# A hybrid encoder layer on one core: the first two projection blocks from scaled rows, the shift's part added in PSUM, and a quarter of the other conditioning sums on GpSimd

## What is computed

```python
cond = silu(c)                                        # 1024 numbers
sh1, sc1, gt1, sh2, sc2, gt2 = split(cond @ ada_w + ada_b, 6)      # ada_w: 1024 x 6144
h = rmsnorm(x, norm1_g) * (1 + sc1) + sh1
q, k, v, feat, gl = split(h @ w_in, ...)              # w_in: 1024 x 4736
# attention from q, k, v; RWKV-7 scan both ways from feat; gates from gl; mix; x = x + gt1 * mixed
h = rmsnorm(x, norm2_g) * (1 + sc2) + sh2
# 16 experts pick 64 tokens each; x = x + gt2 * moe; final rmsnorm
```

## Time and profile before

| | value |
|---|---|
| median of three runs | 1517.89 us |
| the profiled execution | 1520.18 us, span 1518.1 us |
| granted TensorE clock, mean | 0.979 of 2.4 GHz |
| PE busy | 1390.5 us, 92% |
| DVE busy | 445.7 us, 29% |
| ACT busy | 212.5 us, 14% |
| POOL busy | 39.9 us, 3% |
| bytes by DMA | 483.49 MB, mean 318 GB/s |

### The profile page before, as it was taken

The page is one execution under the profiler, slowest core; times in us unless marked ns, Lnnn a source line. Parts: engine busy times, 40 slices in busy tenths (PEclk is TensorE's granted clock), DMA queues, the critical chain, the costliest instruction groups (busy, mean ns, idle before and its releaser), DMA issues.

```text
span 1518.1 us, 21694 instructions
## 1 busy us (share of the span) xinstructions
PE 1390.5 (92%) x9319; PEld 650.0 (43%) x9319; DVE 445.7 (29%) x821; ACT 212.5 (14%) x436; POOL 39.9 (3%) x49
## 2 busy tenths in 40 slices
PE   5999999999999996999999799799799899889897
PEld 2444544445777554343353253253253243243232
DVE  2799554852347314112102102102102101100202
ACT  2035002331332011110010010010010010010011
POOL 2001230000000000000000000000000000000000
PEclk9999999999999997999999999999999999999999
DMA  9954142263215548999999999999999999999996
GB/s 347 371 196 112 56 112 83 84 171 99 83 59 196 192 212 309 364 425 427 428 427 427 428 429 428 428 428 428 428 428 429 428 428 429 429 429 428 428 425 279
DMA packets 95223, 483.49 MB, mean 318 GB/s; under 512 B 36443, under 2 KB 53933, under 8 KB 64949
## 3 DMA queue, kind: packets, MB, share of 16 engines
q1 hardware_dynamic: 95101, 482.49, 78.7%
q10 hardware_dynamic: 56, 0.01, 0.0%
HBM read 470.93 MB, written 10.50 MB: 317 GB/s over the span
## 4 chain that ended last, share of the span: by engine, by line
PE 67%; DMA 26%; DVE 2%; issue 2%; SPq 1%; ACT 1%; POOL 1%; DVEq 0%; POOLq 0%
PE psum L1257 16%; DMA arena<-in_exp_w_up_dram 13%; DMA arena<-in_exp_w_gate_dram 11%; PE psum L651 10%; PE psum L1274 9%; PE psum L739 7%; PE psum L1216 4%; PE psum L1138 3%; PE psum L1054 2%; PE psum L1381 2%; PE psum L1298 1%; SPq L294 1%; DMA arena<-in_ada_w_dram 1%; PE psum L786 1%; PE psum L863 1%
## 5 line engine op out<-in xcount | busy, mean ns | idle before, releaser
L1257 PE MATMUL psum<-arena 128*64 128x512 f32 x2048 | 468.4, 614 | 68.9 <-DMA arena<-in_exp_w_up_dram 51.3
L1257 PEld LDWEIGHTS psum<-arena 128*64 128x64 f32 x2048 | 159.5, 141 | 369.3 <-issue 355.3
L1274 PE MATMUL psum<-arena 128*64 128x512 f32 x928 | 202.7, 593 | 8.0 <-issue 6.5
L651 PE MATMUL psum<-arena 128*128 128x512 f32 x336 | 147.2, 598 | 1.4 <-DVE arena L1762 1.4
L1274 PEld LDWEIGHTS psum<-arena 128*64 128x64 f32 x928 | 76.1, 137 | 126.7 <-issue 126.0
L739 PE MATMUL psum<-arena 128*128 128x512 f32 x256 | 122.0, 610 | 0.0
L651 PEld LDWEIGHTS psum<-arena 128*128 128x128 f32 x336 | 63.8, 192 | 82.2 <-issue 79.5
L2173 DVE TENSOR_TENSOR arena<-arena,psum 128x512 f32<-128x512 f32 x32 | 19.9, 682 | 255.9 <-PE psum L1257 255.9
L2191 DVE TENSOR_TENSOR arena<-psum,arena 128x1024 f32<-128x1024 f32 x7 | 8.6, 1225 | 252.7 <-PE psum L1274 252.7
L2165 DVE TENSOR_TENSOR arena<-arena,psum 128x512 f32<-128x512 f32 x32 | 19.9, 682 | 176.6 <-ACT arena L1650 176.6
L1636 ACT ACTIVATE arena<-psum,arena 128x128 f32<-128x128 f32 x64 | 24.4, 457 | 316.9 <-PE psum L1216 316.9
(11 more groups left out here) (312 smaller groups left out, 1114.3 us busy)
## 6 DMA issues: line engine op xcount, KB each, us to landing
arena<-in_exp_w_gate_dram SPq DMA_DIRECT2D x64, 2048.0 KB, 23.8
arena<-in_exp_w_up_dram SPq DMA_DIRECT2D x58, 2048.0 KB, 26.6
arena<-in_exp_w_down_dram SPq DMA_DIRECT2D x52, 2048.0 KB, 27.0
arena<-in_ada_w_dram SPq DMA_DIRECT2D x24, 1024.0 KB, 9.8
arena<-in_exp_w_down_dram SPq DMA_DIRECT2D x20, 1024.0 KB, 17.8
arena<-in_w_in_dram SPq DMA_DIRECT2D x16, 1024.0 KB, 5.8
arena<-in_exp_w_up_dram SPq DMA_DIRECT2D x12, 1024.0 KB, 6.9
arena<-in_x_dram SPq DMA_DIRECT2D x2, 2048.0 KB, 8.6
```

Source lines behind the costliest of these rows:

```text
L651: ins = mm(bank(b % 4), by(w_ring[g % 2], KC)[:, k, j * P:(j + 1) * P], by(hT, KC)[:, k, :], start=(k == 0), stop=(k == KC - 1))
L1257: ins = mm(bank(4 * kind + n)[e * 64:(e + 1) * 64, :], by(xeT, KC)[:, k, e * 64:(e + 1) * 64], row_half(j + e, r, first)[:, n * 512:(n + 1 ...
L1274: ins = mm(bank(4 + n)[e * 64:(e + 1) * 64, :], by(hidT, FBLK)[:, 4 * kk + b, e * 64:(e + 1) * 64], by(ring[(j + e) % RING], 4)[:, b, n * ...
```

## The change

1. `h_scaled` (x transposed times the scale) is written by DVE without the shift, and blocks 0 and 1 are projected from it. ACT adds the shift and writes `hT`, eight instructions, for blocks 2 and on.
2. SP loads the scale half of `ada_w` first (four loads of 1 MB, 256 rows by 1024 columns each), then `w_in` group 0 into a place of its own, then the four loads of the shift half. PE's `mod_first` takes the scale half alone, 256 columns for each column tile.
3. DVE sums the shift half over its eight row blocks (`shift_sum`), PE adds up over partitions with eight products of one column, DVE adds the bias. DVE then sums `w_in` group 0 weighted by the shift (`bias_sum`, 256 columns, eight instructions), PE adds up with two products of one column, and ACT adds the two results to PSUM banks 0 and 1. `shift(0)` and `shift(1)` wait for it.
4. Pieces 11, 15, 19 and 23 are summed by POOL: four products with a scalar, and two additions of 128 x 2048. The loads of 15, 19 and 23 wait for POOL. DVE keeps twelve pieces. `ada_pool` needs a second set of products with ones, in the same column tiles and banks.
5. On PE, blocks 7 and 8 go ahead of the sums with ones. ACT's `kk_sq` waits for them, since it writes where `ada_pool[0]` lies.
6. All eleven parameter loads (one is new, `ada_b` for shift and scale) are issued by ACT; SP starts with `x`. ACT loads the table for Sqrt ahead of the squares. The four broadcast loads of `ada_b` go.

```diff
-            for r, src in param_rows[:5]:
-                load(par_rows[r:r + src.shape[0], :], src, "params_in")
             load(by(x_in, TT), x[0].rearrange("(t p) d -> p t d", p=P), "x_in")
+            def first_piece(i, o):
+                src = ada_w[0, 2 * i * P:2 * (i + 1) * P, o:o + D].rearrange("(k p) n -> p k n", p=P)
+                load(by(ada_ring[i], 2), src, f"ada_in{i}")
             def ada_piece(n):
-                if n >= 4:
-                    sp.wait_ge(sem("ada_used"), n - 3)
+                if n < 12:
+                    sp.wait_ge(sem("ada_used"), n - 7)
+                elif n >= 12 and n in ADA_POOL:
+                    sp.wait_ge(sem("pool_prep"), ADA_POOL.index(n))
+                elif n >= 12:
+                    sp.wait_ge(sem("ada_used"), 4 + ADA_DVE.index(n - 4) + 1)
...
-            for n in range(KC):
-                ada_piece(n)
-            for q in range(4):
-                load(adab_first[quarter(q), :], ada_b[0:1, 512 * q:512 * (q + 1)].partition_broadcast(32), "first_in")
+            for i in range(4):
+                first_piece(i, D)
             weights(0)
+            for i in range(4):
+                sp.wait_ge(sem("mod_mm"), i + 1)
+                first_piece(i, 0)
             weights(1)
...
+            for q, n in enumerate(ADA_POOL):
+                pool.wait_ge(sem("ada_in3"), 16 * (n // 4 + 1))
+                acc, k = ada_pool[q // 2], n % KC
+                if q == 0:
+                    pool.wait_ge(sem("proj_mm"), 2)
+                    pool.wait_ge(sem("hT_ready"), 2 * KC)
+                    pool.wait_ge(sem("modT_ready"), 4)
+                if q % 2 == 0:
+                    s(nc.gpsimd.tensor_scalar(acc, rest_ring[3], cond[:, k:k + 1], None, ALU.mult))
+                else:
+                    s(nc.gpsimd.tensor_scalar(rest_ring[3], rest_ring[3], cond[:, k:k + 1], None, ALU.mult))
+                    s(nc.gpsimd.tensor_tensor(acc, acc, rest_ring[3], ALU.add))
+                pool.sem_inc(sem("pool_prep"), 1)
...
+                    elif b == 1 and k == 6:
+                        pe.wait_ge(sem("modT_ready"), 2)
+                        for c in range(KC):
+                            ins = mm(bank(4)[:, c:c + 1], shift_sum[:, c * P:(c + 1) * P], ones_wide[:, 0:1], ...)
+                    elif b == 2:
+                        pe.wait_ge(sem("hT_ready"), KC + k + 1)
+                        if k == 6:
+                            pe.wait_ge(sem("modT_ready"), 4)
+                            for c in range(2):
+                                ins = mm(bank(5)[:, c:c + 1], bias_sum[:, c * P:(c + 1) * P], ones_wide[:, 0:1], ...)
...
-            pe.wait_ge(sem("ada_used"), 3 * KC)
+            for b in range(7, 9):
+                project(b)
+            pe.wait_ge(sem("ada_used"), 4 + len(ADA_DVE))
+            pe.wait_ge(sem("pool_prep"), len(ADA_POOL))
...
-                    ins = mm(bank(4 + b)[quarter(q), :], ones_wide, ada_rest[:, o:o + 512], start=True, stop=True)
+                    mm(bank(4 + b)[quarter(q), :], ones_wide, ada_rest[:, o:o + 512], start=True, stop=False)
+                    ins = mm(bank(4 + b)[quarter(q), :], ones_wide, ada_pool[b][:, 512 * q:512 * (q + 1)],
+                             start=False, stop=True)
...
+            act.wait_ge(sem("modT_ready"), 3)
+            for k in range(KC):
+                fn(by(hT, KC)[:, k, :], by(h_scaled, KC)[:, k, :], ACT.Identity, bias=modT[:, k:k + 1]) ...
+            act.wait_ge(sem("modT_ready"), 5)
+            for b in range(2):
+                act.wait_ge(sem("proj_mm"), b + 1)
+                fn(bank(b), bank(b), ACT.Identity, bias=stat[:, 24 + b:25 + b]) ...
...
-                v.tensor_scalar(by(hT, KC)[:, k, :], bank(k % 7 + 1), s1[:, k:k + 1], modT[:, k:k + 1],
-                                ALU.mult, ALU.add).then_inc(sem("hT_ready"), 1)
+                v.tensor_scalar(by(h_scaled, KC)[:, k, :], bank(k % 7 + 1), s1[:, k:k + 1], None, ALU.mult) ...
+            for k in range(KC):
+                piece = by(ada_ring[k // 2], 2)[:, k % 2, :]
+                if k == 0:
+                    s(v.tensor_scalar(shift_sum, piece, cond[:, 0:1], None, ALU.mult))
+                else:
+                    s(v.scalar_tensor_tensor(shift_sum, piece, cond[:, k:k + 1], shift_sum, ALU.mult, ALU.add))
+                if k % 2:
+                    dve.sem_inc(sem("ada_used"), 1)
...
-            n = KC
+            ada(ADA_DVE[0])
+            dve.wait_ge(sem("mod_mm"), 7)
+            v.tensor_copy(stat[:, 24:26], bank(5)[:, 0:2]).then_inc(sem("modT_ready"), 1)
+            n = 1
             for b in range(7):
-                for _ in range((3, 3, 2, 2, 2, 2, 2)[b]):
-                    ada(n)
+                for _ in range((1, 1, 2, 2, 2, 2, 1)[b]):
+                    ada(ADA_DVE[n])
```

More of the change, by code:

```diff
@@ L57 @@
 MU0, MU1, W0, A0, KKC, KAC, RKC, LG, LB, N1, CC = 0, 15, 30, 38, 46, 50, 54, 58, 62, 66, 74
-NPAR = 82
+AB = 82
+NPAR = 98
 class Signal:
@@ L283, in hybrid_layer, with w_home @@
                       (N1, norm1_g.rearrange("l (m p) -> (l m) p", p=P)),
-                      (CC, c.rearrange("l (m p) -> (l m) p", p=P))]
+                      (CC, c.rearrange("l (m p) -> (l m) p", p=P)),
+                      (AB, ada_b[0:1, 0:2 * D].rearrange("l (m p) -> (l m) p", p=P))]
+        ADA_DVE = tuple(n for n in range(KC, 3 * KC) if n % 4 != 3)
+        ADA_POOL = tuple(n for n in range(KC, 3 * KC) if n % 4 == 3)
+        def w_home(g):
+            return w_first if g == 0 else w_ring[g % 2]
         block = ctx.enter_context(nc.Block())
@@ L650, in project @@
                             x_transposed(7)
-                    ins = mm(bank(b % 4), by(w_ring[g % 2], KC)[:, k, j * P:(j + 1) * P], by(hT, KC)[:, k, :],
+                    elif b == 1 and k == 6:
+                        pe.wait_ge(sem("modT_ready"), 2)
+                        for c in range(KC):
+                            ins = mm(bank(4)[:, c:c + 1], shift_sum[:, c * P:(c + 1) * P], ones_wide[:, 0:1],
+                                     start=True, stop=True)
+                        ins.then_inc(sem("mod_mm"), 1)
+                    elif b == 2:
+                        pe.wait_ge(sem("hT_ready"), KC + k + 1)
+                        if k == 6:
+                            pe.wait_ge(sem("modT_ready"), 4)
+                            for c in range(2):
+                                ins = mm(bank(5)[:, c:c + 1], bias_sum[:, c * P:(c + 1) * P], ones_wide[:, 0:1],
+                                         start=True, stop=True)
+                            ins.then_inc(sem("mod_mm"), 1)
+                    ins = mm(bank(b % 4), by(w_home(g), KC)[:, k, j * P:(j + 1) * P],
+                             by(h_scaled if b < 2 else hT, KC)[:, k, :],
                              start=(k == 0), stop=(k == KC - 1))
@@ L1405, in _ @@
             load = lambda dst, src, s: nc.scalar.dma_start(dst, src).then_inc(sem(s), 16)
-            for r, src in param_rows[5:]:
+            for r, src in param_rows:
                 load(par_rows[r:r + src.shape[0], :], src, "params_in")
@@ L1409, in _ @@
             fn(stat[:, 0:KC], pcol[:, CC:CC + KC], ACT.Sigmoid).then_inc(sem("sig_c"), 1)
+            fn(stat[:, 47:48], ident[:, 0:1], ACT.Sqrt)
             act.wait_ge(sem("x_in"), 16)
@@ L1761, in _ @@
                 dve.wait_ge(sem("xT"), k + 1)
-                v.tensor_scalar(by(hT, KC)[:, k, :], bank(k % 7 + 1), s1[:, k:k + 1], modT[:, k:k + 1],
-                                ALU.mult, ALU.add).then_inc(sem("hT_ready"), 1)
+                v.tensor_scalar(by(h_scaled, KC)[:, k, :], bank(k % 7 + 1), s1[:, k:k + 1], None, ALU.mult) \
+                    .then_inc(sem("hT_ready"), 1)
+            for k in range(KC):
+                dve.wait_ge(sem(f"ada_in{k // 2}"), 32)
+                piece = by(ada_ring[k // 2], 2)[:, k % 2, :]
[3 more added lines that the diff above has]
+                    s(v.scalar_tensor_tensor(shift_sum, piece, cond[:, k:k + 1], shift_sum, ALU.mult, ALU.add))
+                if k % 2:
+                    dve.sem_inc(sem("ada_used"), 1)
+            dve.sem_inc(sem("modT_ready"), 1)
+            dve.wait_ge(sem("mod_mm"), 6)
+            v.tensor_tensor(modT[:, 0:KC], bank(4)[:, 0:KC], pcol[:, AB:AB + KC], ALU.add).then_inc(sem("modT_ready"), 1)
+            dve.wait_ge(sem("modT_ready"), 3)
+            dve.wait_ge(sem("w0_in"), 16)
+            for k in range(KC):
+                rows = by(w_first, KC)[:, k, :]
+                if k == 0:
+                    s(v.tensor_scalar(bias_sum, rows, modT[:, 0:1], None, ALU.mult))
+                else:
+                    s(v.scalar_tensor_tensor(bias_sum, rows, modT[:, k:k + 1], bias_sum, ALU.mult, ALU.add))
+            dve.sem_inc(sem("modT_ready"), 1)
             def shift(n):
                 dve.wait_ge(sem("proj_mm"), feature_block(n) + 1)
+                if n < 2:
```

(1 more changed line is left out.)

62 lines of the change are left out of this document (34 added, 28 removed).

## The result

The changed kernel takes 1532.59 us in the median (six runs, 1528.98 to 1533.79), the kernel before on the same chip 1518.54 (1517.29 to 1520.48): a ratio of 1.0088, interval 1.0077 to 1.0099. The prediction said 1518.5 us and at most 1525.5. The profiled execution took 1533.79 us, its span is 1532.0, where before stood 1518.1.

The account below looks back on a forecast made before the run. PE bounds the kernel to block 20, DVE just ahead. PE keeps 1.5 us gain, but DVE, 2.9 later with 2.6 allowed, leaves 0.3, plus 0.3 handoffs: block 20 0.6 later, 1520.8 profiled, 1518.5 median; range 1513.5 to 1525.5.

Parts of the forecast that it names:

- The bound: Up to block 20: DVE becomes the bound, 0.3 us past its slack of 2.6, PE having 1.5 left; chance 0.42.
- Parameters: Start: PE takes the parameters from ACT's queue at 6.7 us, between 6.2 and 9.1; the late end costs up to 2.4.
- the text's own mark of 29 us: First projection: block 0 was to start at 26.9 us; a start after 29 would prove the forecast wrong, through the parameters.
- Shift sums: DVE, blocks 0 and 1: one product of 0.72 and seven sums of 1.2, together 9.4 us, ending at 41.3.
- Clock and one-column products: PE: clock's fall at 36 to 37 us goes despite 2.3 idle; sixteen one-column instructions take 1.8 us, bounds 1.0 and 3.0.
- `w_in` group 3: Blocks 3 to 6: the load is in at 68.3 us, PE wants it at 66.1 and waits 2.2.
- The sums with ones: PE before `kk_sum`: sixteen more instructions take 1.9 us, up to 5.8 if run one after the other.
- POOL's product: POOL's product of a 2048-column piece with a scalar takes 1.95 us, between 1.9 and the addition's 4.53.
- The fourth case: POOL's product is dear: at 4.53 us, 2.6 more, three times gives 7.8, total 1526.3; chance 0.28.
- its mark of 2.8 us: Price per POOL product from which the dear-product case decides: three times 0.8 is 2.4, with 0.6 the tellable 3.0.
- The lock on DVE: DVE with two SBUF inputs stands until POOL's instruction is done; 4.2 us lost at piece 14, 4.1 behind the seventh shift.
- What block 20 gains or loses, the end gains or loses: Attention, scan and experts take data and places from PE's blocks, so block 20's change passes whole to the end.

Follow-up runs that it names:

- no_pool_params: Changed kernel with all sixteen pieces summed by DVE and the first five parameter loads back on SP ahead of `x`: 1522.13 us, 1.0018 of the kernel before.
- after_al: Changed kernel with 187 do-nothing entries more in PE's list, 256 in all against before: 1531.59 us, 1.0084.
- the four kernels with 68 or 69 entries: Changed kernel, its versions with five parameters on SP or POOL's products on ACT, and before plus seventeen one-column products: 1.0088, 1.0068, 1.0042, 1.0039.
- before_pad78: Kernel before with 78 already satisfied waits (39 entries) at the head of PE's list: 1526.1 us, 1.0052.
- before_mm17: Kernel before with seventeen unread one-column products (68 entries) behind the parameters' transposition on PE: 1525.73 us, 1.0039.
- shift_pe_w_al2: Changed kernel without POOL's products, five parameters on SP, eight pieces' shift half on PE, earlier `w_in`, 117 do-nothing entries spread over PE's idle stretches: 1519.08 us, 1.0004.

## Why the prediction was wrong

- **The bound: right by name only.** Between 58 and 137 us the chain of the changed kernel runs through DVE, and its last wait is PE for ACT at `kk`, as the forecast had it. But the forecast had PE 1.5 us early there and DVE 0.3 past its slack, and PE was 9.1 late, most of it without DVE (below).
- **Parameters: the first step that failed.** "I take 6.7", bounds 6.2 and 9.1; it was 10.37, outside. The upper bound let them land no later than `x` (then put at 8.5); they came behind it, and `x` came at 9.28. With 5.38 us for x's transpositions instead of 4.43, block 0 started at 30.50 instead of 26.9, past the text's own mark of 29 us: 2.7 of the 3.6 us are the parameters', 0.95 the transpositions', for which no cause was shown (the granted clock was 1.00 from 20 to 26 us). The sum also has a slip: 6.7, 0.9, 1.28 and 0.2 make 9.1 for the start of the squares and not 10.1, and in the changed kernel they began 2.4 us behind the parameters' transposition, as these terms say. So the parameters cost 3.7 us, and the slip hid 1.0 of them.
- **Shift sums: nearly right.** 10.4 us, from 34.88 to 45.3, for 9.4: 1.30 each instead of 1.2, and a wait of 0.16 after every second.
- **Clock and one-column products: the expectation that the fall goes was wrong.** The sixteen products are 1.95 us at full clock, close to the predicted 1.8, but PE stood idle for 2.26 us ahead of them and the clock was at 0.50 from 45.8 us on, for 6.8 us, and for 3.4 us again from 76.5, behind the wait for `w_in`; before it fell once, for 3.4. (In `no_pool_params`, after a wait of 0.73, it fell too, but at 45.3, behind the products, and for 3.4.) So half of 10.2 us, 5.1, was lost where the forecast had nothing and before lost 1.7; the products took 3.31.
- **`w_in` group 3: right.** A wait of 1.89 for 2.2, but at 75.49 instead of 66, from all the above.
- **The sums with ones: right.** 32 instructions in 3.7 us, from 117.79 to 121.47, twice the 1.9 of 16.
- **POOL's product: the term that was mis-sized most.** 5.44 us for 1.95, and above the upper bound of 4.53. The lower bound was drawn from another kind of instruction, and the estimate of 1.8 us beside it failed with it. The fourth case ("POOL's product is dear", 0.28) named what came true, and its mark of 2.8 us was well passed, but its 1526.3 still priced the product at 4.53 and had nothing else go wrong. DVE lost 13.7 us beside POOL instead of 8.3 and got to L1788's instruction (now L1880) at 109.77 instead of 103.1; without POOL's work `kk` came only 2.6 us sooner.
- **The lock on DVE: right for the additions, in part for the products.** Beside POOL's additions DVE stood until POOL was done. Beside its products a sum ended 0.41 us behind POOL's end and not 2.35. DVE's product with one input in SBUF was held too (5.53 for 1.29). The Trainium skill, "SBUF — State Buffer", "Who interferes with whom", has `tensor_scalar` among the operations that can take the pair of ports DVE shares with GpSimd, and says that the loser blocks fully; this trace agrees for the additions. For the products the second doesn't hold: the sums were nearly done when POOL's product ended.
- **Together:** PE's list alone was 7.5 us late at `kk` (9.1 less the wait of 1.6) and not 1.5 early: the 9.0 between are, as an estimate from the terms above, 3.6 from the start, 1.0 from the shift sums and 5.1 from the clock, less 0.5 for DVE's tiles (5.36 for 5.84), 9.2. DVE added 1.6.
- **"What block 20 gains or loses, the end gains or loses": false.** 4.5 of the 14 us arose in the scan, from where the blocks of PE's code begin: with 187 entries more (`after_al`) they were gone, at a larger lag. No step of the prediction counted the entries of PE's list. The Trainium skill, "Runtime: NRT & Kernel Launch", "Instruction fetch mechanics", says that code comes in blocks of 16 KiB or 256 instructions and that crossing a border is mostly hidden. The 16 KB packets and the 82 gaps at 192 or 193 records past a multiple of 256 agree with the first, and in this scan the second doesn't hold (gaps of up to 3.3 us).

**What stays open:** what makes one border cost nothing and another 3 us (the four kernels with 68 or 69 entries lose 1.7 to 4.5), why POOL's product holds DVE in another way than its addition, why the small loads came in behind `x`, and how much of the loss in front of the scan in `before_pad78` and `before_mm17` is the code load itself, which there fell among the first pieces. In `shift_pe_w_al2` a code load at 22.7 us cost nothing. None of these was tried by itself.

## What to carry to other kernels

In a stretch where PE issues small matmuls without a pause (here 127 of 64 columns in under 4 us), adding or removing a few dozen entries anywhere ahead of it can move the time by more than the change itself; compare the lag ahead of and behind such a stretch before you explain a difference, and pad the list to the old block borders to tell the two apart. When two engines are each late by themselves, undoing one part shows little; undo both before judging either. POOL was a poor place for the SBUF arithmetic of a busy DVE: for the product it took over twice as long as ACT and four times as long as DVE, and DVE lost 13.7 us beside it, more than the 9.6 us of the four pieces it was spared.

## What the runs showed that was not expected

- Waits that have long been met, and do nothing else, took a kernel from 1.0048 to 1.0004 of the one before (1528.63 and 1519.08 us, on two chips) and, in another number, made another one 16.6 us slower (1518.53 to 1535.08).
- POOL's product of 128x2048 with a scalar per partition takes 5.44 us, longer than adding two such tiles (4.50 to 4.71); DVE does it in 1.29, ACT in 2.00. DVE's sums beside it ended 0.41 us behind it, wherever they began.
- Eleven small loads on ACT's queue, issued from 0.81 to 5.3 us, were in only at 10.2 to 10.6, behind the 2 MB of `x` on SP's queue; with five of them issued on SP ahead of `x`, all were in at 5.7 to 6.1.
